# Rows of the cumulated forget gates: a transpose and a broadcast transfer through DRAM in place of four matmuls with ones

## The reference

```python
log_f = jax.nn.log_sigmoid(fa + b_forget[layer])        # (1, 512, 4)
c = jnp.cumsum(log_f, axis=1)
c_keys = c.transpose(0, 2, 1)[:, :, None, :]            # one row of 512 for each head
...
s = jnp.einsum('bqhd,bkhd->bhqk', qn, k) * scale
s = s + cqn[..., None] - c_keys                         # query's own value minus the key's
s = jnp.where(key_idx[None, :] <= qpos[:, None], s, -jnp.inf)
p = jax.nn.softmax(s, axis=-1)
```

## Time and profile before

| | |
|---|---|
| median of 3 runs | 2283.13 us (2282.74 to 2283.80) |
| the profiled execution | 2282.54 us, of which the span from first to last instruction 2280.8 us |
| mean granted clock of TensorE | 0.998 |
| TensorE (PE) busy | 2265.3 us, 99% |
| VectorE (DVE) busy | 1280.7 us, 56% |
| ScalarE (ACT) busy | 883.8 us, 39% |
| DMA engines, mean busy share | 36% |

### The profile page before, as it was taken

How to read it: one execution, slowest core, us unless ns; L and a number is a source line. 1 busy time by engine, 2 the same in 40 slices (tenths; PEclk the granted TensorE clock), 3 DMA queues, 4 the chain that set the end, 5 groups by cost and what they waited for, 6 DMA issues and landing times.

```text
span 2280.8 us, 28255 instructions
## 1 busy us (share of the span) xinstructions
PE 2265.3 (99%) x11178; PEld 1844.8 (81%) x11178; DVE 1280.7 (56%) x2115; ACT 883.8 (39%) x1487; POOL 13.9 (1%) x14
## 2 busy tenths in 40 slices
PE   9999999999999999999999999999999999999998
PEld 7777778878777888788898888888888888888887
DVE  5865655567656556566555544444755536444445
ACT  5444533344445344364343422322322335332233
POOL 0000000000000000200000000000000000000000
PEclk9999999999999999999999999999999999999999
DMA  5655443336644334224353232223222213322231
GB/s 177 176 164 167 141 128 99 100 105 185 175 139 155 97 102 137 81 85 137 102 155 123 94 101 93 92 95 100 93 93 94 92 38 102 97 97 93 93 99 58
DMA packets 122471, 259.64 MB, mean 114 GB/s; under 512 B 12479, under 2 KB 66367, under 8 KB 122212
## 3 DMA queue, kind: packets, MB, share of 16 engines
q1 hardware_dynamic: 122340, 257.84, 36.2%
HBM read 229.73 MB, written 24.13 MB: 111 GB/s over the span
## 4 chain that ended last, share of the span: by engine, by line
PE 97%; DVE 1%; ACT 1%; POOL 0%; issue 0%; DMA 0%; SPq 0%; POOLq 0%; DVEq 0%; ACTq 0%
PE ps L378 28%; PE ps L380 27%; PE ps L379 27%; PE ps L621 2%; PE ps L729 2%; PE ps L404 2%; PE ps L405 2%; PE ps L406 2%; PE ps L1576 1%; PE ps L1515 1%; PE ps L470 1%; ACT t_Tb L190 1%; POOL t_UP L178 0%; PE ps L1013 0%; PE ps L1011 0%; PE ps L1012 0%
## 5 line engine op out<-in xcount | busy, mean ns | idle before, releaser
L378 PE MATMUL ps<-t_P0H,t_whi 128*128 128x512 f32 x1664 | 668.8, 402 | 1.7 <-DVE t_P0L L184 1.7
L380 PE MATMUL ps<-t_P0H,t_wlo 128*128 128x512 f32 x1664 | 656.3, 394 | 0.0
L379 PE MATMUL ps<-t_P0L,t_whi 128*128 128x512 f32 x1664 | 655.2, 394 | 0.0
L190 ACT ACTIVATE t_whi<-t_raw 128x1024 fp32r<-128x1024 f32 (+3 forms) x395 | 404.7, 1028 | 403.9 <-PE ps L380 330.1
L181 DVE TENSOR_TENSOR t_wlo<-t_raw,t_whi 128x1024 fp32r<-128x1024 f32 (+3 forms) x394 | 467.9, 1188 | 40.1 <-PE ps L406 19.9
L378 PEld LDWEIGHTS ps<-t_P0H,t_whi 128*128 128x128 f32 x1664 | 313.5, 188 | 95.5 <-issue 23.3
L380 PEld LDWEIGHTS ps<-t_P0H,t_wlo 128*128 128x128 f32 x1664 | 312.9, 188 | 72.8
L379 PEld LDWEIGHTS ps<-t_P0L,t_whi 128*128 128x128 f32 x1664 | 313.3, 188 | 71.4 <-issue 2.4
L378 PE MATMUL ps<-t_P1H,t_whi 128*128 128x512 f32 (+1 forms) x932 | 361.2, 388 | 0.3 <-DVE t_P1L L181 0.3
L379 PE MATMUL ps<-t_P1L,t_whi 128*128 128x512 f32 (+1 forms) x932 | 359.5, 386 | 0.0
L380 PE MATMUL ps<-t_P1H,t_wlo 128*128 128x512 f32 (+1 forms) x916 | 355.5, 388 | 0.0
(11 more groups left out here) (242 smaller groups left out, 2319.2 us busy)
## 6 DMA issues: line engine op xcount, KB each, us to landing
t_raw<-in_wts SPq DMA_DIRECT2D x362, 512.0 KB, 3.5
far<-t_Tb SPq DMA_DIRECT2D x26, 384.0 KB, 3.0
far<-t_Tb SPq DMA_DIRECT2D x16, 512.0 KB, 3.3
t_PTX<-far SPq DMA_DIRECT2D x64, 96.0 KB, 2.5
t_raw<-in_wts SPq DMA_DIRECT2D x16, 384.0 KB, 3.0
t_QKV<-far SPq DMA_DIRECT2D x32, 128.0 KB, 3.2
t_raw<-in_wts SPq DMA_DIRECT2D x13, 256.0 KB, 2.9
t_PTX<-far SPq DMA_DIRECT2D x24, 128.0 KB, 4.1
```

Source lines behind the costliest of these rows:

```text
L190: return lambda e: e.activation(o, a, f, **k)
L378: e.matmul(bank[:, 0:N], wh, xh, start=first, stop=False)
L379: e.matmul(bank[:, 0:N], wh, xl, start=False, stop=False)
L380: return e.matmul(bank[:, 0:N], wl, xh, start=False, stop=end)
```

## The change

`forget` makes the rows in another way. The cumulated sum stays. VectorE copies it out twice, once with the order of the 16 columns changed to head by head, and once as `cq`. TensorE transposes the reordered 128 x 16 tile to 16 x 128. ScalarE copies that to a temporary tile, a DMA writes it to a DRAM tensor `crow` of the layer (4 rows of 512), and one more DMA, which waits for the first, reads the 2048 numbers to all 128 partitions of `CB`. All four heads then wait for that one DMA.

`gens_A` advances `forget` at every step of `rest` instead of every second. In the forget phase, three steps of the fill come ahead of the attention's first part (`lead=3`); the other phases keep 0.

```diff
             p = op(PE, f, o, free, c_tri, c_ones)
-            o = op(DV, lambda e, bank=bank: e.tensor_copy(cq, bank[:, 0:16]), p)
-            SB.give(bank, o)
-            ftok["cq"] = o
+            byhead = fg[:, 1, :]
+            o = op(DV, lambda e, bank=bank: e.tensor_copy(byhead.rearrange("p (c t) -> p t c", c=4),
+                                                          bank[:, 0:16].rearrange("p (t c) -> p t c", t=4)), p)
+            ftok["cq"] = op(DV, lambda e, bank=bank: e.tensor_copy(cq, bank[:, 0:16]), p)
+            SB.give(bank, ftok["cq"])
+            yield
+            bank, free = SB.take()
+            p = op(PE, lambda e: e.transpose(bank[0:16, 0:128], byhead, ident[:, :]), o, free, c_I)
+            t, free = TMP.take()
+            a = op(AC, act(t[0:16, 0:128], bank[0:16, 0:128], ACT.Copy), p, free)
+            SB.give(bank, a)
+            rows = A["crow"][l:l + 1]
+            w = load(rows[0].rearrange("h (t p) -> (h t) p", p=128), t[0:16, 0:128], deps=[a])
+            TMP.give(t, w)
+            yield
+            w = load(CB.rearrange("p a b -> p (a b)"),
+                     rows.rearrange("a h n -> a (h n)").broadcast_to([128, 2048]), deps=[w])
             for h in range(4):
-                d = diagonal(cq.rearrange("p (t c) -> p c t", t=4)[:, h, :], o)
-                yield
-                ftok[h] = spread_it(d, dst=CB[:, h, :], B=SB)
+                ftok[h] = w
...
-            for n, _ in enumerate(rest()):
-                if n % 2:
-                    next(steps, None)
+            for _ in rest():
+                next(steps, None)
                 yield
...
-            drive(attention(units(kind, tk, npair, q, k, v), gate_y(slots, zslots, ztok), by_dma=True), fill, num, den)
+            drive(attention(units(kind, tk, npair, q, k, v), gate_y(slots, zslots, ztok), by_dma=True), fill, num, den,
+                  lead=3 if kind == "forget" else 0)
...
+    A["crow"] = nc.dram_tensor("crow", (2, 4, 512), _mybir.dt.float32).ap()
```

More of the change, by code:

```diff
@@ L1924, in build_program @@
         T["ps"] = ctx.enter_context(nc.psum_tensor("ps", [128, 8, 512], F32))
-        T["s_c"] = [sem(f"s_c{i}") for i in range(44)]
+        T["s_c"] = [sem(f"s_c{i}") for i in range(48)]
         T["s_w"] = [sem(f"s_w{i}") for i in range(NRAW)]
```

## The result

The changed kernel takes 2287.12 us (median of 22 runs, 2284.92 to 2288.34) against 2283.10 for the kernel before (22 runs). The ratio is 1.0016, 95% interval 1.001 to 1.0022: 4.0 us slower by the medians (2.3 to 5.0 by the interval), within the 0.2% of the forecast, and in its range. The forecast was 2285.2, 2.1 us slower.

A forecast was written before the change was run, and what follows sets the result against it. TensorE bounds the kernel, busy 2265.3 of 2280.8 us. Per layer -3.44 + 0.25 + 2.8 + 0.6 = +0.2, two layers +0.4, one clock fall +1.7: +2.1 on 2283.13, forecast 2285.2 us, range 2281.5 to 2289.

The forecast's parts named there:

- What is removed: On TensorE, four L470 matmuls of 512 columns go from each layer, 0.86 us each, 3.44 us a layer.
- The transpose: One transpose added on TensorE per layer, taken at 0.25 us, bounds 0.21 and 0.58; no wait for its operand.
- The wait before L983: TensorE waits for the gate chain before the cumulated sum, now behind four steps, not eight: 2.8 us a layer (2.6 to 3.2).
- Rival 2: The gate chain follows the order, so no wait before L983; -2.6 us a layer, 2277.9 us, 0.23% faster; chance 0.07.
- The lead: Three steps moved forward are missing at the forget phase's end; TensorE waits 0.6 us a layer before the last value product.
- The clock: TensorE's clock may halve for 3.4 us behind each layer's wait, costing 1.7 us; one fall in two taken as likeliest.
- rival 3: The clock falls in both layers and stays halved longer, twice 3.4 us each; 2290.3 us, slower; chance 0.10.
- DMA: The rows' small write and 1 MB read stay hidden: landing at 54.6, needed by VectorE at 56.4, 1.8 us to spare.
- The reserve behind late rows: Late rows hold up VectorE, but reach TensorE only when a weight chunk's 5.6 us of reserve are used up.
- Rival 4: Rows land after 62, VectorE stands, and each microsecond beyond costs TensorE one; 2289.5 us at 19 us round trip; chance 0.03.

The follow-up runs named there:

- late-sum run: Changed kernel, but the forget gates' parts begin four steps later, so the cumulated sum stands behind eight steps again; 2276.70 us, ratio 0.9976 to the kernel before.
- run of the kernel before with the early sum: Kernel before with only the cumulated sum's place changed: first four forget-gate parts at the first four steps, rows by matmuls with ones; 2290.90 us, ratio 1.0037.
- run with the late sum and lead 2: Changed kernel, forget gates' parts begun four steps later, and a lead of two steps instead of three; 2281.05 us, ratio 0.9995 to the kernel before.
- The early read: As the run with the late sum and lead 2, but the 1 MB read takes cosine-table rows, issued some 7 us earlier; 2276.23 us, ratio 0.9973.

## Why the prediction was right, and where it was off

The direction, the place and the sizes of the terms came out nearly as worked out, but for the clock. The total is 1.9 us off: the clock's term is about 2.4 us too small, and the other terms, 0.5 us too large over two layers, hide a part of that by luck. Point by point:

- **What is removed.** 3.44 us a layer. The records of L470 are gone from both stretches. The late-sum run agrees as a whole: -5.6 expected, -6.0 measured.
- **The transpose.** Taken at 0.25 us, measured 0.12. It has one record here, not two, and it undercuts the lower bound of 0.21, which came from the rate of the float32 matmul L470.
- **The wait before L983.** Predicted 2.79 us, measured 2.75 and 2.74. The chain of Exp, table load and Ln was not drawn along by the new order: its idle time of 1.35 us before the last operation is the same to the hundredth. Rival 2 falls.
- **The lead.** Predicted 0.6 us a layer, measured 0.50 in both.
- **The clock.** This is the term that was mis-sized. The mechanism was right, but I counted one fall in two waits as likeliest, and the profiled execution has two. From the medians, 4.0 us less the -0.1 of the other terms is 4.1, or 2.4 falls of 1.7. The mean granted clock of the executions gives the same figure without the sum: it is 0.99645 over the 22 of the changed kernel and 0.99825 over the 24 of the kernel before that were timed beside the first experiments, and 0.0018 of 2283 us are 4.1 us. The run of the kernel before with the early sum shows how the mean can exceed two: some falls last 6.8 us and cost 3.4, as rival 3 had it, others don't come. The one fall of 3.4 us in the earlier trace rows was too little to size a mean, and that it shows there at all is partly chance. The same wait of 1.98 us before L705 stands in all 14 profiled executions; nine have 3.4 us at half clock behind it, and five, the late-sum run among them, have none (windows of that run, the wait ends at 974.17):

```profile
974.00:975.00 1.00, 0.82 (x5) 0.77 (x6) 0.96 (x5) 0.05 (x1) 0.00 (x0) 1.00 0.88 307
975.00:976.00 1.00, 1.00 (x5) 0.56 (x3) 0.68 (x3) 1.00 (x3) 0.00 (x0) 1.00 0.34 135
```

So two profiled executions can differ by 1.7 us for a reason that is not the change, and a count of falls in one of them is a sample. The Trainium skill, "TensorE: Matmul & The Clock Gate", section "The HAM clock gate", says that the clock is halved after idleness. It ties this to how long the idleness lasts, which the prediction left out when it had both waits pay by that rule alone. The rows here show a fall in both layers of the changed kernel and none in one layer of two in two other runs; what the time shows is a price for each such wait of about 2 us on average (4.1/2).
- **DMA.** Hidden, as predicted. The read is issued at 47.00 and lands within 4.7 us, at 51.7; I had 54.6 (the terms that I gave, 46.1, 3.0 and 5.0, make 54.1). VectorE needs it at 57.7. The bound of 3.0 us for the small write held here (1.4) and not in the late-sum run (3.5).
- **The reserve behind late rows.** This was wrong, though it didn't matter for the changed kernel. Rival 4 said that TensorE is reached only when rows land 5.6 us late. In the run with the late sum and lead 2, VectorE starts 1.8 us late in layer 0 and 2.5 in layer 1, and TensorE waits 4.2 us before L404. The early read takes away 4.8 us. How two microseconds of lateness become these waits was not followed step by step. It is not that VectorE has no free time: from 478 to 555 us it is busy for 57.1 of 77 us. But it plays its queue in order, and ahead of the lo part that TensorE misses at 545.05 stand operations that themselves wait for transfers (VectorE's timeline of that run):

```profile
522.86 1.25 DVE L599 STREAM_TRANSPOSE t_PTb<-t_PTX 128x1024 f32<-128x1024 f32 x1 [2.68 <-DMA t_PTX<-far]
...
534.25 0.69 DVE L178 TENSOR_TENSOR t_QKV<-t_QKV,t_TMP 128x512 f32<-128x512 f32 x1 [1.56 <-DMA t_TMP<-t_TMP]
...
543.82 1.18 DVE L181 TENSOR_TENSOR t_wlo<-t_raw,t_whi 128x1024 fp32r<-128x1024 f32 x1
```

So the expected gain of the change, 6.6 us of TensorE's time (3.32 in each layer), is real. It was given back through the moved sum (5.5 us), the falls that follow (about 4) and the lead (1.0).

Left open: why one wait is followed by a fall and the next, equally long, isn't. Why the lead of three, with rows as late as with two (1.80 and 2.53 us against 1.78 and 2.47), costs so much less was not settled either: the two runs have 1.0 and 4.2 us before L404. The waits account for 2.3 of the 4.4 us between them (3.2 more before L404, 0.9 less before the last value product), and the mean granted clock of the executions (0.9985 against 0.9979) for roughly another 1.4.

## What to carry to other kernels

When a step is moved forward in the queue of the engine that bounds the kernel, ask what its operand's chain was timed against: this one had been covered to within a tenth of a microsecond, and moving its place four steps forward turned all four steps into a wait. A wait on TensorE may cost more than its length, since the clock can fall behind it. The 14 profiled executions have 28 waits of 1.76 us or more by the page's count; 18 are followed by 3.4 us at half clock, two by 6.8 and eight by none, which is 1.3 us lost on average. Shorter waits, the last ten microseconds of the program aside, brought one fall, behind the pair of 1.21 and 0.81 us shown above. A cost that comes by chance is sized from medians of many executions and not from one trace. A transfer that is off the path must still land before the engine that feeds the path needs it: with a shortfall of two microseconds there, TensorE's longest wait came some sixty microseconds later.

## What was not expected of the hardware

The small write of 8 KB landed in 1.4 us in the changed kernel but in 3.5 us in the late-sum run. In the latter a weight fetch of 512 KB is issued 0.4 us before it on the same queue (SP's timeline of that run):

```profile
47.09 0.33 SPq L218 DMA_DIRECT2D t_raw<-in_wts  x1
47.47 0.42 SPq L200 DMA_DIRECT2D crow<-t_TMP  x1
50.95 0.34 SPq L200 DMA_DIRECT2D t_M<-crow  x1
```

The changed kernel has no such neighbour (45.62 for the write, 47.00 for the read). That the fetch delays the write fits the rows, but it was not tried by itself.

The clock fell when TensorE was already at work again: two microseconds after the wait in the changed kernel (at about 45.6 behind 43.33), and 0.3 us after it in the run with the early sum (at about 43.8 behind 43.52).
